# Keys and values of the dilated attention computed in the early column pairs and kept in DRAM; the order of one quad's vector work

## What is computed

```python
h = layer_norm(x, emb_ln_g, emb_ln_b)                       # (1, 256, 4096)
proj = h @ w_in                                             # w_in: 4096 x IN_WIDTH
q_a, kv_a, dq, dk, dv, g_mla, g_dswa, r_mla, r_dswa = split(proj)
#  1024   576  3072 3072 3072  2048   1024    4096   4096   columns
a = mla_attention(q_a, kv_a, ...)                           # 16 heads, dense
y_mla = (a * silu(g_mla)) @ w_o_mla
b = dilated_mixture(dq, dk, dv, rel_bias)                   # 3 groups of 8 heads of 128, dilations 1, 4, 16
y_dswa = (b * silu(g_dswa)) @ w_o_dswa
merged = sigmoid(r_mla) * y_mla + sigmoid(r_dswa) * y_dswa
out = layer_norm(2 ** 0.25 * h + merged @ w_out, ln_g, ln_b)
```

## Time and profile before

| what | value |
|---|---|
| median of three runs | 2748.84 us |
| the profiled execution | 2749.5 us |
| its span, first to last instruction | 2747.7 us |
| PE (matmuls) busy | 2712.5 us, 12628 instructions |
| DVE busy | 1723.4 us, 1788 instructions |
| ACT busy | 1220.0 us, 1329 instructions |
| read from / written to DRAM | 525.78 MB / 11.61 MB, 196 GB/s |

### The profile page before, as it was taken

How to read it: one execution, slowest core, us unless ns; L and a number is a source line. 1 busy time by engine, 2 the same in 40 slices (tenths; PEclk the granted TensorE clock), 3 DMA queues, 4 the chain that set the end, 5 groups by cost and what they waited for, 6 DMA issues and landing times.

```text
span 2747.7 us, 34908 instructions
## 1 busy us (share of the span) xinstructions
PE 2712.5 (99%) x12628; PEld 2263.9 (82%) x12628; DVE 1723.4 (63%) x1788; ACT 1220.0 (44%) x1329; POOL 92.6 (3%) x145
## 2 busy tenths in 40 slices
PE   7999999999999999999999999999999999999998
PEld 5988888888888899888888888888888888888886
DVE  7778888888864577545454654545465555656556
ACT  4445545454554455434343433434344333543333
POOL 0000000000000011000000000000000000000000
PEclk9999999999999999999999999999999999999998
DMA  6656566565576534666666666666666666677765
GB/s 202 194 200 223 201 213 225 204 226 208 193 208 194 162 121 139 188 191 174 191 183 191 189 191 176 188 182 191 183 195 214 220 216 205 192 235 226 228 217 173
DMA packets 248180, 539.30 MB, mean 196 GB/s; under 512 B 16202, under 2 KB 32950, under 8 KB 248037
## 3 DMA queue, kind: packets, MB, share of 16 engines
q1 hardware_dynamic: 238160, 506.52, 58.7%
q0 software_dynamic: 8656, 28.49, 3.9%
q10 hardware_dynamic: 1224, 2.44, 0.2%
HBM read 525.78 MB, written 11.61 MB: 196 GB/s over the span
## 4 chain that ended last, share of the span: by engine, by line
PE 95%; DMA 2%; DVE 2%; issue 0%; ACT 0%; SPq 0%; DVEq 0%; ACTq 0%
PE acc L552 23%; PE acc L554 23%; PE acc L553 23%; PE bank L559 3%; PE bank L561 3%; PE bank L560 3%; PE acc L559 3%; PE acc L561 3%; PE acc L560 3%; DMA q_raw<-in_w_in 1%; PE acc L657 1%; PE acc L658 1%; PE acc L665 1%; PE bank L732 1%; PE bank L782 1%; PE bank L766 1%
## 5 line engine op out<-in xcount | busy, mean ns | idle before, releaser
L1162 DVE TENSOR_TENSOR w_lo<-w_raw,w_hi 128x1024 fp32r<-128x1024 f32 (+3 forms) x768 | 894.2, 1174 | 750.6 <-ACT w_hi L908 747.0
L908 ACT ACTIVATE w_hi<-w_raw 128x1024 fp32r<-128x1024 f32 (+3 forms) x768 | 769.8, 1015 | 793.0 <-PE acc L554 762.7
L552 PE MATMUL acc<-w_hi,oper_hi 128*128 128x512 f32 (+1 forms) x2352 | 913.6, 388 | 0.9 <-DVE w_lo L1162 0.8
L554 PE MATMUL acc<-w_hi,oper_lo 128*128 128x512 f32 (+1 forms) x2352 | 904.5, 385 | 0.0
L553 PE MATMUL acc<-w_lo,oper_hi 128*128 128x512 f32 (+1 forms) x2352 | 903.8, 384 | 0.1
L554 PEld LDWEIGHTS acc<-w_hi,oper_lo 128*128 128x128 f32 x2352 | 441.5, 188 | 88.2 <-issue 0.3
L552 PEld LDWEIGHTS acc<-w_hi,oper_hi 128*128 128x128 f32 x2352 | 441.8, 188 | 85.8 <-DVE w_lo L1162 1.8
L553 PEld LDWEIGHTS acc<-w_lo,oper_hi 128*128 128x128 f32 x2352 | 442.0, 188 | 84.4
L950 ACT ACTIVATE q_hi<-q_raw 128x2048 fp32r<-128x2048 f32 x112 | 214.7, 1918 | 263.6 <-DVE q_raw L1239 198.9
L1245 DVE TENSOR_TENSOR q_low<-q_raw,q_hi 128x2048 fp32r<-128x2048 f32 x112 | 252.4, 2284 | 22.1 <-ACT q_hi L950 22.1
L559 PE MATMUL bank<-q_hi,oper_hi 128*128 128x512 f32 x365 | 142.4, 390 | 4.0 <-DVE q_low L1245 4.0
(11 more groups left out here) (301 smaller groups left out, 2628.4 us busy)
## 6 DMA issues: line engine op xcount, KB each, us to landing
w_raw<-in_w_in SPq DMA_DIRECT2D x448, 512.0 KB, 4.3
q_raw<-in_w_in SPq DMA_DIRECT2D x112, 1024.0 KB, 4.9
w_raw<-in_w_out SPq DMA_DIRECT2D x128, 512.0 KB, 3.7
w_raw<-in_w_o_mla SPq DMA_DIRECT2D x64, 512.0 KB, 3.9
w_raw<-in_w_o_dswa SPq DMA_DIRECT2D x32, 512.0 KB, 3.9
w_raw<-in_w_q_b SPq DMA_DIRECT2D x32, 384.0 KB, 3.6
w_raw<-in_w_in SPq DMA_DIRECT2D x32, 288.0 KB, 3.3
w_raw<-in_w_kv_b SPq DMA_DIRECT2D x32, 256.0 KB, 2.8
```

The lines of the kernel that those rows point to most:

```text
L552: pe.matmul(y, hi[:, k, tok(t)], wh, start=first, stop=False)
L554: ins = pe.matmul(y, lo[:, k, tok(t)], wh, start=False, stop=last)
L908: act.activation(w_hi[:, n % RING, 0:w], w_raw[:, n % RING, 0:w], ACT.Copy).then_inc(w_hi_ready, 1)
L1162: dve.tensor_tensor(w_lo[:, n % RING, 0:w], w_raw[:, n % RING, 0:w], w_hi[:, n % RING, 0:w].bitcast(F32), ALU.subtract).then_inc(w_lo_read ...
```

## The change

Six more column pairs run ahead of the seven of the gates: the 3072 columns of the keys and the 3072 of the values, which lie side by side in `w_in`. Their twelve results are stored in DRAM by POOL without a sigmoid (`blocks_d`, 26 blocks; in the old file `gates_d`). The twelve K and V chunks leave the section "dswa": its turn now has four chunks, Q1, Q2, the gate and the next Q0, with the sides `att0`, `att1`, `att2` and `mix`. Each `att` chunk first takes q from the chunk before (`evacuate` at slot 0), transposes K and q together at slot 1 (16 transposes, four banks), copies them at slot 2, and does its heads two slots later than before (scores at slots 3, 6, 9, 12; the last product with v at 15). K and V of a group are loaded by POOL, 512 KB each, between its bias loads, into `dk_sb` (new, it lies on `gate_sb`) and `dv_sb`. The K load of the next group waits until K is transposed; the V load waits until the last product with v of the group before; the first K load of the second turn waits for the merge of the first.

One order is changed: at q = 3 of every pair but the first, DVE does `quad_low(3)` ahead of `quad_sums(4)`. Names of semaphores and of the DRAM tensor change with it, and the waits that counted pairs of gates use `GATE_PAIRS`. Left out of the diff are these, the declaration of `dk_sb`, and the removal of the `qT` and `kT` branches on PE, ACT and DVE.

```diff
@@ -55,9 +55,11 @@
-PAIRS = 7
+KV_PAIRS, GATE_PAIRS = 6, 7
+PAIRS = KV_PAIRS + GATE_PAIRS
 QUADS = KT // 2
-PAIR_COL = COL_RM + CW
+PAIR_COLS = [COL_DK + 2 * CW * n for n in range(KV_PAIRS)] + [COL_RM + CW + 2 * CW * n for n in range(GATE_PAIRS)]
+K_BLOCK, V_BLOCK, RM_BLOCK, RD_BLOCK = 0, KV_PAIRS, 2 * KV_PAIRS, 2 * KV_PAIRS + GATE_PAIRS
 SEVEN = tuple(range(2, QUADS - 1, 2))
@@ -142,8 +144,6 @@
             body.append(full(COL_DQ + c, CW, f"att{g - 1}"))
-        body.append(full(COL_DK + c, CW, f"qT{g}"))
-        body.append(full(COL_DV + c, CW, f"kT{g}"))
     body.append(full(COL_GD, CW, f"att{NG - 1}"))
@@ -504,7 +506,7 @@
                         sp.wait_ge(quad_done, g - RAWS + 1)
-                    rows = w_in[0][2 * q * P:(2 * q + 2) * P, PAIR_COL + p * 2 * CW:PAIR_COL + (p + 1) * 2 * CW]
+                    rows = w_in[0][2 * q * P:(2 * q + 2) * P, PAIR_COLS[p]:PAIR_COLS[p] + 2 * CW]
                     sp.dma_start(q_raw[g % RAWS].rearrange("p (a i) n -> p a (i n)", a=2),
@@ -739,15 +741,15 @@
-            def heads_T(src, i, j, free):
...
-                if j in (1, 2):
-                    if j == 1:
-                        pe.wait_ge(acc_free, free)
+            def heads_T(g, i, free):
...
+                pe.wait_ge(acc_free, free)
+                pe.wait_ge(dk_loaded, at(i, 16 * NG, 16 * (g + 1)))
+                for n, (src, bank) in enumerate(((dk_sb, bA), (dk_sb, bB), (a_sb, bC), (a_sb, bD))):
                     for hh in range(2):
                         for t in range(TT):
-                            h = 2 * (j - 1) + hh
-                            ins = pe.transpose(BK[j - 1][:, hh * SEQ + t * P:hh * SEQ + (t + 1) * P],
+                            h = 2 * (n % 2) + hh
+                            ins = pe.transpose(bank[:, hh * SEQ + t * P:hh * SEQ + (t + 1) * P],
                                                src[:, t, h * HD:(h + 1) * HD], ident)
@@ -755,8 +757,10 @@
                 head = lambda h: at(i, NG * QUAD, g * QUAD + h)
+                if j == 1:
+                    heads_T(g, i, free)
                 for h in range(QUAD):
-                    if j == 3 * h + 1:
+                    if j == 3 * h + 3:
                         bank = BK[h % 2]
@@ -765,17 +769,17 @@
                         ins.then_inc(dscores, 1)
-                    if j == 3 * h + 3:
+                    if j == 3 * h + 5:
                         pe.wait_ge(dprobs_ready, head(h) + 1)
...
                         ins.then_inc(dprobsT_ps, 1)
-                    if j == 3 * h + 4:
+                    if j == 3 * h + 6:
                         pe.wait_ge(dprobsT_ready, head(h) + 1)
                         if h == 0:
-                            pe.wait_ge(acc_free, free)
+                            pe.wait_ge(dv_loaded, at(i, 16 * NG, 16 * (g + 1)))
                         for t in range(TT):
@@ -972,7 +972,7 @@
                     quad_high(g)
-                    if p and q == 2:
+                    if p > KV_PAIRS and q == 2:
                         gate_pair(p - 1)
@@ -1018,16 +1018,20 @@
                 kw = SEQ if g == 0 else P
+                if j == 2:
+                    for n, (dst, bank) in enumerate(((dkT, bA), (dqT, bC))):
+                        act.wait_ge(dT_ps, at(i, 4 * NG, 4 * g + 2 * n + 1))
+                        act.activation(dst[:, 0:2, :], bank[:, :].rearrange("p (a b) -> p a b", a=2), ACT.Copy).then_inc(dTA_ready, 1)
                 for h in range(QUAD):
                     n1 = at(i, NG * QUAD, g * QUAD + h + 1)
-                    if j == 3 * h + 1:
+                    if j == 3 * h + 3:
                         act.wait_ge(dnegmax, n1)
...
                         ins.then_inc(dprobs_ready, 1)
-                    if j == 3 * h + 3:
+                    if j == 3 * h + 5:
                         act.wait_ge(dprobsT_ps, n1)
@@ -1275,11 +1273,14 @@
                     p, q = g // QUADS, g % QUADS
-                    if g + 1 < NQ and is_seven(g + 1):
+                    sums_late = p > 0 and q == SEVEN[0] + 1
+                    if g + 1 < NQ and is_seven(g + 1) and not sums_late:
                         quad_sums(g + 1)
...
                     quad_low(g)
+                    if sums_late:
+                        quad_sums(g + 1)
                     if p and q == 0:
@@ -1371,17 +1372,21 @@
                 kw = SEQ if g == 0 else P
+                if j == 2:
+                    for n, (dst, bank) in enumerate(((dkT, bB), (dqT, bD))):
+                        dve.wait_ge(dT_ps, at(i, 4 * NG, 4 * g + 2 * n + 2))
+                        dve.tensor_copy(dst[:, 2:4, :], bank[:, :].rearrange("p (a b) -> p a b", a=2)).then_inc(dTB_ready, 1)
                 for h in range(QUAD):
...
                     n1 = at(i, NG * QUAD, head + 1)
-                    if j == 3 * h + 4:
+                    if j == 3 * h + 6:
                         dve.wait_ge(do_ps, n1)
...
                     n1 = at(i, NG * QUAD, head + 1)
-                    if j == 3 * h + 1:
+                    if j == 3 * h + 3:
                         dve.wait_ge(dscores, n1)
@@ -1753,10 +1749,13 @@
             for p in range(PAIRS):
-                dst = gates_d[2 * p:2 * p + 2].rearrange("i p t n -> p i t n")
+                dst = blocks_d[2 * p:2 * p + 2].rearrange("i p t n -> p i t n")
                 for n, (piece, c) in enumerate(((dst[:, 1, 1, :], c_sb[3]), (dst[:, 1, 0, :], c_sb[2]), (dst[:, 0, :, :], c_first[:, :, :]))):
-                    pool.wait_ge(c_gated, 3 * p + n + 1)
-                    pool.dma_start(piece, c).then_inc(gates_stored if n else fourth_stored, 16)
+                    if p < KV_PAIRS:
+                        pool.wait_ge(c_done, 4 * p + (1, 2, 4)[n])
+                    else:
+                        pool.wait_ge(c_gated, 3 * (p - KV_PAIRS) + n + 1)
+                    pool.dma_start(piece, c).then_inc(blocks_stored if n else fourth_stored, 16)
             pool.wait_ge(rows_stored, 16)
@@ -1771,20 +1770,32 @@
             pool.wait_ge(am_lo_ready, MLA_HEADS // 2)
-            for quad in range(GH // QUAD):
-                for head in range(NG * QUAD):
-                    load_bias(quad, head)
+            pool.wait_ge(fourth_stored, 16 * PAIRS)
+            pool.wait_ge(blocks_stored, 32 * PAIRS)
+            units = [(quad, g) for quad in range(GH // QUAD) for g in range(NG)]
+            for u, (quad, g) in enumerate(units):
+                for h in range(QUAD):
+                    load_bias(quad, g * QUAD + h)
+                    if h == 1:
+                        if u:
+                            pool.wait_ge(do_ps, QUAD * u)
+                        pool.dma_start(dv_sb[:, :, :], blocks_d[V_BLOCK + 2 * g + quad]).then_inc(dv_loaded, 16)
+                    if h == 1 and g == 0:
+                        if quad:
+                            pool.wait_ge(mix_ready, quad)
+                        pool.dma_start(dk_sb[:, :, :], blocks_d[K_BLOCK + quad]).then_inc(dk_loaded, 16)
+                    if h == 2 and g + 1 < NG:
+                        pool.wait_ge(dT_ps, 4 * u + 2)
+                        pool.dma_start(dk_sb[:, :, :], blocks_d[K_BLOCK + 2 * (g + 1) + quad]).then_inc(dk_loaded, 16)
             pool.wait_ge(mix_ready, GH // QUAD)
-            pool.wait_ge(fourth_stored, 16 * PAIRS)
-            pool.wait_ge(gates_stored, 32 * PAIRS)
-            for n in range(PAIRS):
+            for n in range(GATE_PAIRS):
                 if n:
                     pool.wait_ge(merged, n)
-                pool.dma_start(sig_d[:, :, :], gates_d[PAIRS + n]).then_inc(sig_d_loaded, 16)
+                pool.dma_start(sig_d[:, :, :], blocks_d[RD_BLOCK + n]).then_inc(sig_d_loaded, 16)
                 pool.wait_ge(acc_free, SEC["merge0"].chunk0 + 2 * n + 1)
-                pool.dma_start(sig_m[:, :, :], gates_d[n]).then_inc(sig_m_loaded, 16)
+                pool.dma_start(sig_m[:, :, :], blocks_d[RM_BLOCK + n]).then_inc(sig_m_loaded, 16)
             first = SEC["out0"].slot0
...
             pool.wait_ge(merged, D // CW)
```

More of the change, by code:

```diff
@@ L270, in program @@
     group_c = nc.inline_tensor(np.repeat(np.eye(NG, dtype=np.float32), GH, axis=1), name="group_const").ap()
-    gates_d = nc.dram_tensor("merge_gates", (2 * PAIRS, P, TT, CW), F32).ap()
+    blocks_d = nc.dram_tensor("pair_blocks", (2 * PAIRS, P, TT, CW), F32).ap()
     bias_rows_d = nc.dram_tensor("bias_rows", (NG * GH, PITCH), F32).ap()
@@ L331, in program @@
         gate_sb = sb("gate_sb", R_C + 28 * K, [P, TT, CW])
+        dk_sb = sb("dk_sb", R_C + 28 * K, [P, TT, CW])
         mT = sb("mT", R_C, [P, KT, SEQ])
@@ L415, in program @@
                              "b_hi_ready", "b_lo_ready"))
+        dk_loaded, dv_loaded = sem("dk_loaded"), sem("dv_loaded")
         bias_loaded = [sem(f"bias_loaded{n}") for n in range(2)]
@@ L424, in program @@
         (t_step, t_made, t_hi_ready, t_lo_ready, sum_step, sums_ready, q_hi_ready, q_lo_ready, quad_done, p1_out, u_done, c_done,
```

(23 more changed lines are left out.)

## The result

The changed kernel takes 2718.88 us (median of four runs, 2714.57 to 2719.88), the kernel before 2748.82 us. The ratio is 0.9888, 95% interval 0.9876 to 0.9901. The forecast was 2713.3 us with a range of 2710.8 to 2723.0. Two more groups of runs gave medians of 2717.6 and 2718.2 us. The twelve runs of the changed kernel spread over 5.6 us (2714.41 to 2720.00). The kernel before spread over half a microsecond in its first four runs and over 2.7 us in all of them (2747.27 to 2749.93). The wider spread is part of what had to be explained.

What follows compares the result with a forecast made beforehand. PE's matmuls and stalls were taken to bound the kernel: 2749.5 - 28.6 (fewer matmuls) - 8.8 (stall at quad 3) + 1.8 (late quad 5) = 2713.9 us, so 2713.3 for the median; range 2710.8 to 2723.

Steps and rivals of the forecast that it cites:

- What bounds the kernel, and the 28.6 us: PE's matmul count bounds the kernel; six pairs replacing twelve K/V chunks save 126 matmuls at 0.2267 us, 28.6 us.
- The stall at q = 3, 8.8 us: At pair boundaries, low part of quad 3 ahead of quad 4's sums removes PE's six waits: 8.8 us off.
- What is late next: At twelve pair boundaries, quad 5's low part, behind quad 6's sums, comes late: 0.15 us each, +1.8 us; ends 0 to 8.4.
- Loads and stores in the pairs: In K/V pairs, stores a microsecond earlier move away from quad 4's load, 0.9 us lower, or leave the time unchanged.
- Attention in fewer chunks: In the dilated section, denser attention chunks still cover their copies and splits: 0 us, at most some 9 us.
- K and V from DRAM: In the attention chunks, POOL's K and V loads land well before PE wants them: 0, with 0 to 2 us for late weights.
- rival B: Attention chunks too dense, PE idle at slots 1 or 3: 1.5 us in each of six, 2722.3 us; chance 0.12.
- A: At pair boundaries the wait only moves to quads 4 and 5: 1.5 us at each of twelve, 2729.5 us; chance 0.07.
- C: In attention chunks, K/V loads on POOL's queue come late, PE waits at slot 6 or 1: 2755 us, slower; chance 0.03.

Runs made afterwards that it cites:

- kernels with late stores: POOL waits until quad 6 of the next pair is done before storing a pair's results: changed kernel 2709.7 us, with old order 2709.8, kernel before 2738.8.
- the kernel with the copies: Changed kernel, but ACT copies each piece of a K/V pair onto itself before POOL stores it, about a microsecond later: 2716.6 us, ratio 0.9883.

## Why the prediction was right, and which term was mis-sized

*What bounds the kernel, and the 28.6 us.* Right. 126 matmuls fewer. In the kernels with late stores a pair takes 82.28 us, which is 363 x 0.2267. The two distances of matmuls carried this term alone.

*The stall at q = 3, 8.8 us.* Right: no loss at quad 3 at any boundary of the changed kernel. Undone, it came back with 24.0 us.

*"What is late next", 12 x 0.15 = 1.8 us.* The step named the right quad and the right chain, and its size was off by a factor of five: 9.3 us, more than the 8.4 I had set as the upper end. This is the mis-sized term. Three things were wrong in it. I took half of boundary 5 as typical, though each boundary loses whatever one of two loads is late, and the kernel before had hidden that behind its stall; in the kernel with the order edit alone the six boundaries lost 0.5 us each. I let the K/V pairs be no worse than the gates, though boundaries 1 to 5 lost 0.41 to 1.55 us each. And the upper end of 0.7 was one boundary's value: boundary 9 alone lost 3.5.

*"Loads and stores in the pairs": the earlier K/V stores move away from the load of quad 4, or leave the time as it is.* Wrong. The store of `c_first` goes out 5.6 us into the pair (423.96, pair 3 at 418.37), in the moment in which quad 0 ends and frees the buffer for quad 4; at gate boundaries it goes out 6.7 us in. Quad 4 landed at 12.6 to 13.8 us at boundaries 1 to 5. The Trainium skill, "DMA: Bandwidth & Descriptors", Queues, rings and completion order, says that an engine takes turns between the queues that have work. The traces agree as far as they can: the load lands at 10.2 to 10.6 us without the store (boundary 9 left out) and at 12.1 and more with it (at 11.5 to 11.7 at boundary 7, where the store goes out at 7.8, and once at boundary 6). What I drew from it, quad 4 landing sooner at K/V boundaries and 0.9 us less, had the wrong sign for the landing, for I had not put the two issue times side by side. On the time no sign is shown: the kernel with the copies can't be told from the changed one.

*Attention in fewer chunks, K and V from DRAM.* Right but for one wait of 1.0 us, late in the first `att0` chunk of the first turn (at 1680 us), where ACT gets a weight tile late. A wait at this place stands in eight of the nine profiles with the moved keys and values (0.5 to 1.0 us; not in that of the copies), and none in the second turn. It is not at the slots that rival B named. I did not test it, and its cause stays open.

*The sum, against the profiled execution.* Forecast 2713.9, measured 2718.2, so 4.3 us more. 9.3 - 1.8 = 7.5 at the boundaries and 1.1 in the attention. Against that stand 3.8 us in parts that the prediction did not cost: the first quad starts at 170.35 and not at 171.80 (it varies from 170.4 to 171.5 over the experiments), the start of the gates waits 0.8 us less, and the last stage took 1.5 us less. That leaves 0.5 us without a name. The last part is no chance: a wait of 1.2 us near the end of the kernel (PE at L884, for DVE's `resid`) stands in all three profiles without the moved keys and values and in none of the nine with them. Why is open. That the time came out well inside the range is partly luck: without these 3.8 us the median would be 2722.6 us, and the upper end of the range, 2723, was set for rival B, which did not happen.

*The rivals.* A, that the wait only moves, with 1.5 us at each boundary, was half right: the wait did move to quads 4 and 5, with 0.8 us at each on average. Its sign, a wait of over 1 us, stood at two of the twelve boundaries, 3 and 9. B and C did not happen; K and V landed in 5.1 us, the first two in 8.2 and 9.7.

## What to carry to other kernels

A stall hides the slack behind it: before removing one, follow the chain of the engine that was late until it has idle time again, and look at how the landing times on which it hangs vary. If that landing shares its stretch with a store that nobody waits for, move the store out of the stretch first: here one wait on POOL's queue gave 9.7 us in the kernel before and 8 us after the change (2709.7 us, the fastest version, 1.4% below the kernel before), and made the order edit needless. And if sums feed another engine whose result comes back, leave an independent instruction between them and that result.

## What was unexpected of the hardware

A 512 KB store that starts within about a microsecond of a 1 MB load delays the landing of that load by 1.4 to 3.5 us (11.7 to 13.9 us after the pair's start in place of 10.3), and the delay is not the same from one place to another: boundary 3 lands at 13.7 to 13.9 us in all three profiles of the changed kernel, boundary 6 at 11.7 to 12.3. At boundary 9 all but the last part of the load had landed by 12.8 us and the last came at up to 15.9; even with late stores, it was the latest there (12.3 against 10.3). One thing is special about that place: in all nine profiles with the moved keys and values a single packet of 16 KB on another queue, marked "instruction", starts 5.6 to 6.2 us into the pair, together with the load of quad 4, and takes 0.9 to 1.6 us. At no other boundary does one start between 4.8 and 9.7 us. It is no proof. With late stores and the old order the packet is there too and the load lands at 10.6 us, and no run moved it.

The half clock after a wait of 2.08 us, in the kernel with the order edit undone, was the other surprise: a stall can cost more than its own length, here 1.6 us more.
